# Seven-product matrix chunks: partial sums kept in three PSUM banks, with products added in place

## The reference

```python
def swiglu(h, w_gate, w_up, w_down):
    return (jax.nn.silu(h @ w_gate) * (h @ w_up)) @ w_down
...
        x = x + 0.5 * swiglu(rms_norm(x, norm_g[layer, 0]), ffn_w_gate[layer, 0], ffn_w_up[layer, 0], ffn_w_down[layer, 0])
```

## Time and profile before

| | us |
|---|---|
| time, median of 3 runs | 2085.79 (2085.78 to 2086.21) |
| the profiled execution's own time | 2080.56 |
| its span, first to last instruction | 2078.8 |
| TensorE busy | 2048.7 (99%) |
| VectorE busy | 1469.5 (71%) |
| ScalarE busy | 807.6 (39%) |
| GpSimd busy | 549.0 (26%) |

### The profile page before, as it was taken

How to read it: one execution, slowest core, us unless ns; L and a number is a source line. 1 busy time by engine, 2 the same in 40 slices (tenths; PEclk the granted TensorE clock), 3 DMA queues, 4 the chain that set the end, 5 groups by cost and what they waited for, 6 DMA issues and landing times. The chain is left out here.

```text
span 2078.8 us, 34375 instructions
## 1 busy us (share of the span) xinstructions
PE 2048.7 (99%) x13914; PEld 2013.1 (97%) x13914; DVE 1469.5 (71%) x2292; ACT 807.6 (39%) x1342; POOL 549.0 (26%) x382
## 2 busy tenths in 40 slices
PE   8999999999999999999999999999999999999998
PEld 6999999999889999999999999999999999999998
DVE  6886675963655678667586778485776878666685
ACT  5343332442433334333244344243344534333343
POOL 4342332402000034233240233242310035233230
PEclk9999999999999999999999999999999999999999
DMA  5223232343121222323233213323242123323222
GB/s 154 67 82 92 72 97 66 82 105 95 46 61 42 72 67 81 92 72 97 67 82 108 61 57 91 93 61 94 69 124 76 41 67 82 87 76 92 72 56 82
DMA packets 312004, 165.16 MB, mean 79 GB/s; under 512 B 15339, under 2 KB 309431, under 8 KB 311848
## 3 DMA queue, kind: packets, MB, share of 16 engines
q1 hardware_dynamic: 309152, 158.36, 27.8%
q0 software_dynamic: 2576, 4.57, 1.0%
q10 hardware_dynamic: 120, 0.04, 0.0%
HBM read 158.94 MB, written 4.00 MB: 78 GB/s over the span
## 5 line engine op out<-in xcount | busy, mean ns | idle before, releaser
L495 PE MATMUL psum<-xg_hi,in_hi 128*128 128x320 f32 x1952 | 611.4, 313 | 2.9 <-DVE in_lo L1197 2.4
L497 PE MATMUL psum<-xg_hi,in_lo 128*128 128x320 f32 x1952 | 604.5, 310 | 0.0
L496 PE MATMUL psum<-xg_lo,in_hi 128*128 128x320 f32 x1952 | 604.4, 310 | 0.0
L495 PE MATMUL psum<-f_hi,f_out_hi 128*128 128x320 f32 x1408 | 437.1, 310 | 12.3 <-DVE x L1240 7.7
L497 PE MATMUL psum<-f_hi,f_out_lo 128*128 128x320 f32 x1408 | 435.7, 309 | 0.0
L496 PE MATMUL psum<-f_lo,f_out_hi 128*128 128x320 f32 x1408 | 435.7, 309 | 0.0
L495 PEld LDWEIGHTS psum<-xg_hi,in_hi 128*128 128x128 f32 x1952 | 367.5, 188 | 9.1 <-issue 3.3
L496 PEld LDWEIGHTS psum<-xg_lo,in_hi 128*128 128x128 f32 x1952 | 367.9, 188 | 0.6
L497 PEld LDWEIGHTS psum<-xg_hi,in_lo 128*128 128x128 f32 x1952 | 367.7, 188 | 0.0
L1641 POOL TENSOR_TENSOR sums<-in_raw 128x512 f32<-128x512 f32 x72 | 103.7, 1441 | 738.6 <-DVE in_lo L1209 481.6
L495 PEld LDWEIGHTS psum<-f_hi,f_out_hi 128*128 128x128 f32 x1408 | 264.9, 188 | 14.4 <-issue 8.4
(11 more groups left out here) (201 smaller groups left out, 2863.7 us busy)
## 6 DMA issues: line engine op xcount, KB each, us to landing
in_raw<-in_ffn_w_gate SPq DMA_DIRECT2D x88, 512.0 KB, 4.0
in_raw<-in_ffn_w_up SPq DMA_DIRECT2D x88, 512.0 KB, 5.3
out_raw<-in_ffn_w_down SPq DMA_DIRECT2D x96, 384.0 KB, 3.4
out_raw<-in_ffn_w_down SPq DMA_DIRECT2D x32, 256.0 KB, 2.9
in_raw<-in_mix_w_in SPq DMA_DIRECT2D x14, 512.0 KB, 5.2
out<-y_nat SPq DMA_DIRECT2D x5, 512.0 KB, 3.2
x_nat<-in_x_prompt SPq DMA_DIRECT2D x4, 512.0 KB, 5.4
in_raw<-in_mix_w_in SPq DMA_DIRECT2D x8, 256.0 KB, 4.8
```

Of the source, the lines that this page charges most:

```text
L495: pe.matmul(dst, w_hi, v_hi, start=first, stop=False)
L496: pe.matmul(dst, w_hi, v_lo, start=False, stop=False)
L497: return pe.matmul(dst, w_lo, v_hi, start=False, stop=last)
```

## The change

The three banks of a chunk are now (0, 1, 2) or (3, 6, 7) in turn (`CHUNK_BANKS[s % 2]`). The order of products is B11, T2, B21, T3, T1, T4, B22 with weight slots 0, 2, 1, 3, 4, 5, 6. B21 is added by TensorE onto the bank that still holds B11 (no new start of the accumulation), T3 and then T4 onto the bank of T2, B22 onto the bank of T1. In between the partial contents are read: B11 by ScalarE (`p1`) before B21 may begin, T2 by VectorE (`u2`) before T3, T2+T3 (`t2a`) before T4, T1 (`t2a` again) before B22. VectorE has five additions per chunk. The gate of the low half is B11+B21 as it stands in the bank, and Silu reads it there. TensorE waits before the first product of every fast chunk for `x_updated` of all earlier `out` units (`used`); before, the wait stood at the fifth product. ScalarE's first high split for the next chunk waits for three products of this one instead of two.

```diff
-        PRODUCTS = ["B11", "B21", "T2", "T3", "T1", "T4", "B22"]
-        PRODUCT_BANK = [0, 1, 2, 3, 6, 7, 5]
+        PRODUCTS = [("B11", 0, 0, False), ("T2", 2, 1, False), ("B21", 1, 0, True), ("T3", 3, 1, True),
+                    ("T1", 4, 2, False), ("T4", 5, 1, True), ("B22", 6, 2, True)]
+        CHUNK_BANKS = ((0, 1, 2), (3, 6, 7))
...
                 for k in range(4):
-                    end = product(psum[:, bank, 0:HALF], w_hi[:, k], w_lo[:, k], hi[:, k], lo[:, k], k == 0, k == 3)
+                    pe.matmul(dst, w_hi[:, k], hi[:, k], start=first and k == 0, stop=False, skip_group_check=True)
+                    pe.matmul(dst, w_hi[:, k], lo[:, k], start=False, stop=False, skip_group_check=True)
+                    end = pe.matmul(dst, w_lo[:, k], hi[:, k], start=False, stop=last and k == 3, skip_group_check=True)
...
                     if p == 0:
-                        wait(pe, p1_done, s)
-                    elif s > 0:
-                        pe.wait_ge(evac_done, 7 * (s - 1) + (1, 2, 3, 5, 6, 7)[p - 1])
-                    if p >= 4:
                         wait(pe, x_updated, used)
-                    part(bank, p, b)
+                        wait(pe, gate_done, 2 * s - 3)
+                    elif p == 1:
+                        wait(pe, evac_done, 5 * s - 6)
+                    elif p == 2:
+                        pe.wait_ge(p1_done, s + 1)
+                    elif p == 3:
+                        pe.wait_ge(evac_done, 5 * s + 1)
+                    elif p == 4:
+                        wait(pe, evac_done, 5 * s - 5)
+                    elif p == 5:
+                        pe.wait_ge(evac_done, 5 * s + 2)
+                    else:
+                        pe.wait_ge(evac_done, 5 * s + 3)
+                    part(CHUNK_BANKS[s % 2][bank], slot, b, not more, p in (2, 5, 6))
...
-                                if g and i == 0 and (j, half) == (1, 0) and k == 0:
-                                    pe.wait_ge(evac_done, 7 * fast_chunk(index, f0 + gk - 1) + 7)
...
-                    act.wait_ge(prod_mm, 7 * s - 5)
+                    act.wait_ge(prod_mm, 7 * s - 4)
                 fast_hi_split((0, 2), raw_blocks(n % 2, 0, 2))
...
-                        wait(act, evac_done, 7 * s - 5)
-                        act.activation(p1[:, :], psum[:, 0, 0:HALF], ACT.Copy).then_inc(p1_done, 1)
+                        wait(act, evac_done, 5 * s - 1)
+                        act.activation(p1[:, :], psum[:, CHUNK_BANKS[s % 2][0], 0:HALF], ACT.Copy).then_inc(p1_done, 1)
                         if i > 0:
                             hidden_split(i - 1, 1, u, 0)
-                        act.wait_ge(evac_done, 7 * s + 1)
-                        act.activation(t1[:, 0], t1[:, 0], ACT.Silu).then_inc(gate_done, 1)
+                        act.wait_ge(prod_mm, 7 * s + 3)
+                        wait(act, hidden_done, u - 1)
+                        act.activation(t1[:, 0], psum[:, CHUNK_BANKS[s % 2][0], 0:HALF], ACT.Silu).then_inc(gate_done, 1)
...
+            def ups_begun(s, u, lows):
+
                 dve.wait_ge(p1_done, s + 1)
-                evacuate(t1[:, 0], 1, p1[:, :], s, 1, 1)
...
+                evacuate(u2[:, :], 1, p1[:, :], s, 2)
                 for split in lows:
                     fast_lo_split(*split)
-                dve.wait_ge(evac_done, 7 * s + 2)
-                evacuate(t2b[:, :], 3, u2[:, :], s, 3, 3)
+                wait(dve, hidden_lo, u)
+                evacuate(t2a[:, :], 1, p1[:, :], s, 4)
...
-                evacuate(t2a[:, :], 6, t2b[:, :], s, 4, 4)
-                evacuate(u2[:, :], 6, u2[:, :], s, 4, 5)
+                dve.wait_ge(evac_done, 5 * s + 2)
+                evacuate(t2a[:, :], 2, t2a[:, :], s, 5)
                 for split in lows:
                     fast_lo_split(*split)
-                dve.wait_ge(evac_done, 7 * s + 4)
-                evacuate(t2b[:, :], 7, t2b[:, :], s, 5, 6)
+                evacuate(t2b[:, :], 1, p1[:, :], s, 6)
```

More of the change, by code:

```diff
@@ L583, in out_unit, with part @@
                 last.then_inc(out_mm, 1)
-            def part(bank, slot, b):
+            def part(bank, slot, b, first, last):
                 hi, lo, _ = block_parts[b]
                 w_hi, w_lo = (weight_slots(w, slot, slot + 1)[:, 0].rearrange("p (k c) -> p k c", k=4) for w in (in_hi, in_lo))
+                dst = psum[:, bank, 0:HALF]
                 for k in range(4):
-                    end = product(psum[:, bank, 0:HALF], w_hi[:, k], w_lo[:, k], hi[:, k], lo[:, k], k == 0, k == 3)
+                    pe.matmul(dst, w_hi[:, k], hi[:, k], start=first and k == 0, stop=False, skip_group_check=True)
+                    pe.matmul(dst, w_hi[:, k], lo[:, k], start=False, stop=False, skip_group_check=True)
+                    end = pe.matmul(dst, w_lo[:, k], hi[:, k], start=False, stop=last and k == 3, skip_group_check=True)
                 end.then_inc(prod_mm, 1)
             def fast_in(s, fresh, used):
-                for p, (b, bank) in enumerate(zip(PRODUCTS, PRODUCT_BANK)):
-                    if p in (0, 2, 4, 6):
-                        pe.wait_ge(fast_split, 4 * s + p // 2 + 1)
+                for p, (b, slot, bank, more) in enumerate(PRODUCTS):
+                    if p in (0, 1, 4, 6):
+                        pe.wait_ge(fast_split, 4 * s + (1, 2, 0, 0, 3, 0, 4)[p])
                     if fresh is not None:
@@ L937, in gate_high @@
             def gate_high(s):
-                act.wait_ge(evac_done, 7 * s + 7)
+                act.wait_ge(evac_done, 5 * s + 5)
                 act.activation(t1[:, 1], t1[:, 1], ACT.Silu).then_inc(gate_done, 1)
@@ L1262, in rows_out, with evacuate, gate_high @@
                                   row_rstd[lo:hi, tile:tile + 1], None, ALU.mult).then_inc(rows_right, 1)
[L1264 to L1269, removed]
-                dve.wait_ge(p1_done, s + 1)
-                evacuate(t1[:, 0], 1, p1[:, :], s, 1, 1)
[L1273 to L1279, removed]
+            def evacuate(to, bank, more, s, p):
+                dve.wait_ge(prod_mm, 7 * s + p)
+                dve.tensor_tensor(to, psum[:, CHUNK_BANKS[s % 2][bank], 0:HALF], more, ALU.add).then_inc(evac_done, 1)
+            def gate_high(s):
+                evacuate(t1[:, 1], 2, u2[:, :], s, 7)
+            def ups_begun(s, u, lows):
+                dve.wait_ge(p1_done, s + 1)
+                evacuate(u2[:, :], 1, p1[:, :], s, 2)
                 for split in lows:
                     fast_lo_split(*split)
-                dve.wait_ge(evac_done, 7 * s + 2)
-                evacuate(t2b[:, :], 3, u2[:, :], s, 3, 3)
+                wait(dve, hidden_lo, u)
+                evacuate(t2a[:, :], 1, p1[:, :], s, 4)
             def ups(s, u, lows):
-                dve.wait_ge(evac_done, 7 * s + 3)
-                wait(dve, hidden_lo, u)
-                evacuate(t2a[:, :], 6, t2b[:, :], s, 4, 4)
-                evacuate(u2[:, :], 6, u2[:, :], s, 4, 5)
+                dve.wait_ge(evac_done, 5 * s + 2)
+                evacuate(t2a[:, :], 2, t2a[:, :], s, 5)
                 for split in lows:
                     fast_lo_split(*split)
-                dve.wait_ge(evac_done, 7 * s + 4)
-                evacuate(t2b[:, :], 7, t2b[:, :], s, 5, 6)
+                evacuate(t2b[:, :], 1, p1[:, :], s, 6)
                 dve.wait_ge(gate_done, 2 * s + 1)
-                dve.wait_ge(evac_done, 7 * s + 6)
+                dve.wait_ge(evac_done, 5 * s + 4)
                 dve.tensor_tensor(t2b[:, :], t2b[:, :], t1[:, 0], ALU.mult).then_inc(hidden_done, 1)
@@ L1368, in ffn @@
                             hidden_split(i - 1, 1, u, 0)
-                        wait(dve, hidden_done, u - 1)
-                        gate_low(s)
-                        ups_begun(s, early[0:1])
+                        ups_begun(s, u, early[0:1])
                         ups(s, u, early[1:2])
```

2 lines of the change are left out of this document (1 added, 1 removed).

## The result

The changed kernel takes 2143.53 us (median of 4 runs, 2138.2 to 2145.99) against 2085.78 us. The ratio is 1.0276, with a 95% interval of 1.0252 to 1.0300. The profiled execution took 2138.2 us with a span of 2136.4, 57.6 us longer than the span before.

What follows compares the result with a forecast made beforehand. TensorE, busy in 2048.7 of 2078.8 us, was taken to bound the kernel. Waits for p1 (38.9 us) and x (14.6 us) sum to 53.5; added to 2085.8 they give 2139 us, range 2108 to 2168.

Steps and rivals of the forecast that it cites:

- The bound: Fast chunks: TensorE is busy 73.92 of 73.92 us per group, so nothing can be won there.
- Nothing for adding in place: Products added onto a bank already holding one: cost 0, with the restart after a wait as upper end.
- The wait for p1: Third product, four boundaries in each of 12 groups: TensorE stalls for ScalarE's copy, 48 x 0.81 = 38.9 us.
- The chain's links: VectorE's second low split through GpSimd's sums, high gate and slot 6 split to the p1 copy: all 0.83 us earlier.
- the first rival: Fast chunks: GpSimd's first sum comes after VectorE's multiplication, p1 is early, only x waits stay; 2100 us, chance 0.12.
- The wait for x: First product of each group waits for the last out unit's update: 4 x 1.95 and 8 x 0.85, 14.6 us.
- the release: Group start: time from the x update's end to TensorE's restart, taken as 0.06 us.
- The waits inside the chunk: T4 waits for T2+T3 to be read: 3.31 against 3.52 us, hidden; a 0.1 us miss costs 12 us.
- T3's wait: Inside a chunk, T3 waits for T2's addition: about 1.5 us against 1.76, so hidden.
- Sum and base: Whole kernel: 53.5 us added to the timed 2085.8, which lies an unexplained 5.2 us above the profiled execution: 2139.
- a rival of 79 us at 0.05: Each of 48 boundaries draws a half-clock stretch of 3.3 us: 79 us more, 2219; chance 0.05.
- What would show it: Changed kernel's profile: TensorE busy near 2049 us, 12 x waits, 48 p1 waits, VectorE about 70 us less busy.

Runs made afterwards that it cites:

- the run with both moved: Changed kernel with x wait in a group's second chunk, p1 copied before the previous high gate, u2 added before slot 6's low split: 2086.85 us, ratio 1.0016.
- The run with the later x wait: Changed kernel with the x wait at the second product of a group's second chunk instead of the first chunk's first product: 2124.38 us, ratio 1.0200.

## Why the prediction was right, point by point

**The bound.** No time was to be won in fast chunks, and none was; with all waits moved away the time is that of before and a little more.

**Nothing for adding in place.** Between waits the matmuls start 0.1467 us apart as before; in the group without delays of the run with both moved, the 504 matmuls take 73.92 us, though 24 of its 42 products are added onto a bank that holds another. The upper end that I gave it, a restart, wasn't reached.

**The wait for p1.** Predicted 48 waits, none in a group's first and last chunk, 0.81 us each; measured 48 at these places, 0.84 on average. 40 are at 0.68 + 0.11 = 0.79, near enough; 8 are longer, up to 1.09 + 0.11. The average is near by a little luck, as the 40 lie 0.8 us in all under the sum and the 8 together 2.4 us over it. In seven of the 8 GpSimd's first sum starts 0.34 to 0.56 us after the low split's end instead of 0.14, and what released it is the landing of the raw weights, 0.06 to 0.07 us before; at the other boundaries the sum starts 0.14 or 0.15 us after the split. One of the seven:

```profile
845.59 1.29 POOL L1647 TENSOR_TENSOR sums<-in_raw 128x512 f32<-128x512 f32 x1 [5.47 <-DMA in_raw<-in_ffn_w_up]
```

In the eighth VectorE's addition behind T1 itself starts 0.37 us late (1271.19), for a reason that the trace doesn't show. The chain's links stood to within 0.05 us at the other 40. The experiments bear out each: without blocking no stall, with one more addition 0.40 more.

The run with the later x wait also holds, once in 48, the first rival's case: a late landing put the first sum behind the start of the multiplication.

```profile
2015.44 0.49 DVE L1306 TENSOR_TENSOR t2b<-t2b,t 128x320 f32<-128x320 f32 x1
2015.73 1.36 POOL L1648 TENSOR_TENSOR sums<-in_raw 128x512 f32<-128x512 f32 x1 [5.93 <-DMA in_raw<-in_ffn_w_up]
```

The multiplication took 0.49 us, and the third product lost 0.05 us instead of 0.68. The hidden values' second multiplication then met a sum instead, 1.57 us long, and the fourth product waited 0.8. So the rival's mechanism is real, but VectorE's freed time didn't bring it about, and in this one case the wait was handed on.

**The wait for x.** Predicted 14.6 us, measured 15.3. The term that was mis-sized is the release in a block's first group: 0.25 us after the update's end in three of four, not 0.06.

**The waits inside the chunk.** I called T4's the closest, with 0.2 us to spare, and so it is in the changed kernel: in all 60 chunks but the groups' last its releaser ends 0.28 us before it starts, 0.06 of release and 0.22 to spare. It bound only in the run with both moved, where the split that it hangs on met a sum. T3's wait, 1.5 against 1.76 by my sum, I had worked out only behind a late `p1`, where it holds (0.32 us from the releaser's end to the start). With the copy early it is the next to bind, as the links behind `gate_high` on VectorE don't move with the copy.

**Sum and base.** 53.5 us predicted, 55.7 found in the trace, 57.75 by the medians. The last 2 us are the clock's, net, which I had only as a rival of 79 us at 0.05. It happened, small, and at none of the 48 boundaries. I had also read the clock before too kindly. It was still 1.00 during the wait of 1552.00 to 1556.00, but fell right behind it:

```profile
1556.00:1560.00 4.00, 4.00 (x19) 4.00 (x18) 2.50 (x6) 0.93 (x2) 0.00 (x0) 0.57 0.29 85
```

The 5.2 us between profiled and timed runs, which I couldn't name, go with the clock too: executions of the kernel before with a mean granted clock of 0.998 took 2080.4 to 2081.3 us, those with 0.995 2085.5 to 2086.0. The changed kernel took 2138.2 and 2141.2 us at 0.995 and 2145.8 and 2146.0 at 0.992.

**What would show it.** TensorE's busy time rose to 2065.7 and didn't stay near 2049: its matmuls last 0.31 us from start to end and start 0.147 apart, so the first 0.16 us of each wait count as busy, and so do a restart and the half clock. VectorE lost 57 us, not 70: successive instructions overlap by 0.08 us, 144 x 0.40. Both were the wrong way to read "busy", and neither stood in the sum.

## What to carry to other kernels

When one engine is busy all through, an edit that reuses a buffer within the loop buys nothing and puts a deadline on whoever reads that buffer: look up in the trace when the reader ends now, even if nobody waits for it yet, and what is queued ahead of it. A bank that comes round once per chunk gives its reader a whole chunk; one that is written again two products later gives it 1.8 us, and everything queued in front of it counts. Moving the reader ahead shows the next such deadline, so follow all of them before counting a gain.

## What the runs showed that I had not expected

**Just arriving costs too.** A releaser that ends just before TensorE arrives still makes the second matmul late. In the run with both moved, VectorE's addition of T2+T3 and the sixth product that it releases:

```profile
278.58 0.48 DVE L1283 TENSOR_TENSOR t2a<-psum,p 128x320 f32<-128x320 f32 x1
279.11 0.42 PE L595 MATMUL psum<-mix_hi,in_hi 128*128 128x320 f32 x1
279.37 0.31 PE L596 MATMUL psum<-mix_lo,in_hi 128*128 128x320 f32 x1
```

The later the releaser, the more is lost. By the fourth and sixth products of this run, from the releaser's end to the product's start and what the second matmul lost: 0.055 us, 0.10; 0.09 us, 0.07; 0.11 us, 0.055; 0.13 us, 0.03; 0.17 us and more, nothing, but for three first chunks with 0.01 to 0.025 at 0.2. The list of waits shows nothing of these; only the distances between starts do.

**Waits and the clock.** Windows of the changed kernel around a group's start at 1761.48, which waited 1.9 us:

```profile
1757.00:1761.40 4.40, 2.60 (x18) 2.33 (x16) 4.40 (x8) 1.38 (x3) 3.87 (x2) 1.00 0.02 5
1762.10:1765.50 3.40, 3.40 (x15) 3.40 (x14) 1.95 (x2) 0.44 (x1) 2.68 (x2) 0.50 0.08 15
1765.50:1770.00 4.50, 4.50 (x33) 4.50 (x32) 0.52 (x2) 1.39 (x2) 0.00 (x0) 1.00 0.82 223
```

The clock falls to 0.50, its lower level of 1.2 GHz, after TensorE was busy in 2.60 of 4.40 us, stays there for 3.4 us of full work and returns. Behind the same wait in the three other blocks it stays at 1.00. In the stretch the matmuls start 0.27 us apart instead of 0.147 (1762.16, 1762.43, 1762.70), so each microsecond of it costs at most half.

Before the last 10 us of each trace, the time at half clock was 6.8 us in the kernel before, 6.8, 6.8, 3.4 and 6.8 in the four kernels with no new stall, and 13.7, 13.7, 17.1, 20.5, 17.1 and 23.9 in the six with stalls. But that isn't the new stalls' doing alone. I set every stretch of the eleven traces beside the waits, by the starts of the matmuls. Of 35 waits of 2.6 to 2.8 us, all of them also in the kernel before, 13 have a stretch that begins at most 0.6 us before or 1.0 after their end; of 16 new ones of 1.6 to 2.05 us (the first group of a block, in four kernels) 3 have; of 300 of 0.35 to 1.6 us, the waits for `p1` and `u2` among them, none. The other eleven stretches, one per trace, lie at one place, behind small matmuls of 128 and of 1 column (at 1593.9 in the kernel before), and are 3.4 to 10.2 us long. So of the changed kernel's 60 new waits one has a stretch at its end. Why the long old waits and that place have more of it in the six kernels isn't known; these are single executions, and three of the four kernels without new stalls have lost the three long waits for `x` as well. The Trainium skill's "TensorE: Matmul & The Clock Gate", section "A second HAM failure mode: psum-queue depth-cycling", says that short idle gaps between groups of matmuls make the clock swing. The traces agree for 16 of the 51 waits of 1.6 us and more, and for none of the 300 shorter ones.
